# Seven products instead of eight in the last down projection of every feed-forward block

## The chip, the cores and the metric

One core of one Trainium2 chip runs the whole program. The metric is device time in microseconds (us); the kernel before takes 2784.4 us in the median of three runs (2784.36 to 2786.01). The profiled execution took 2784.26 us, of which the profile's span, from the first to the last instruction, is 2782.7 us.

## The reference

A trunk of two layers works on 640 tokens (512 of one new stream, 16 of each of eight running streams) with 1024 features. Every layer is

```python
x += 1/2 * SwiGLU_a(RMSNorm(x))        # hidden width 2816
x += mixer(RMSNorm(x))                 # layer 0: retention, layer 1: stick-breaking attention
x += 1/2 * SwiGLU_b(RMSNorm(x))
x += sigmoid(RMSNorm(x) @ W_gate) * (p[i] @ W_proj)
```

and a final RMSNorm follows. SwiGLU is `(silu(a) * b) @ w_down` with `a, b = split(x @ w_gu)`. All of it is float32.

## The kernel before

**Layout.** The residual stream `x` stays on the chip as eight tiles of 128 features by 640 tokens; a token half is 320 columns. A float32 matrix product is made of three passes over high and low parts: every operand is split by the scalar engine (high part, rounded, L1078 and the like) and the vector engine (low part, the difference), and the tensor engine multiplies high by high, high by low and low by high. One matmul instruction covers a 128x128 weight block and 320 columns. The phases are `ffn, ret, ffn, ple, ffn, sb, ffn, ple`: four feed-forward blocks, each followed by another kind of phase.

**A feed-forward block** runs through its 22 hidden tiles in groups of 4, 6, 6 and 6 (`PIECES`, L38). Each group makes its gate and up tiles and then adds its share of the down projection to `x`. In groups 1 to 3 the gate and up products go by Winograd's form of Strassen's scheme: seven products of quarter matrices instead of eight. Groups 1 and 2 do the same in the down projection (`SEVEN_DOWN`, L50). There a *job* (kind `dn`) is one pair of output tiles d and d+1: seven products of 9 matmuls each, so four jobs per group. Group 0 and, in this kernel, the last group do the down projection plainly: eight output tiles of 36 matmuls each (in the last group L751 to L755, a loop of two rounds).

**The order in a down job** is written by hand. With `d` the job, `old` the one before it and `new` the one after it, the tensor engine runs: product 1 of d, product 3 of old, 2 and 6 of d, 4 of old, 5 and 7 of d (L643 to L706). Product 2 waits for `snap1` (scalar engine, product 1 copied to a second bank), product 6 for `lo56` (vector engine, low parts of two weight sums), product 7 for `snap2`, product 3 for `lo34`, product 4 for `c22` (the first of the vector engine's four additions into `x`: c22, c11, c12, c21). The scalar engine's queue in a job is snap1, hi12 of new, snap2, hi34 of d, hi56 of new, hi7 of new (L1229 on). The vector engine's is c22 of old, lo56 and lo7 of d, c11 and c12 of old, the weight sums s1 to s3 of new, c21 of old, lo12 and s4 of new, lo34 of d (L1940 on). Each engine runs its queue in order.

**The hand-over to the next phase.** The last group's additions give the final `x`. In the plain form each finished tile is at once split for the next phase (`feed`, L1099: `feed_hi`, then `square`; `feed_lo` on the vector engine, L1732), and GpSimd adds the squares up in `ssum` (`add_squares`, L1593). The squares pass through the two-slot buffer `sq`, which lies over the end of the low parts of the hidden tiles. The next phase begins with matmuls on its slot-0 weights; these are split (`split_hi`, `split_lo`) at the end of the feed-forward block. Then `sum_squares` (L564) sums over the partitions, which needs all eight squares added. It stands behind 48 matmuls in `ret` and `sb` and behind 36 in `ple`, where the products with the layer's input embedding come first. `sb` starts only when every bank of the feed-forward block has been read.

Of the kernel before, what the change touches and what calls it, by code (L numbers as in the profile page):

```python
# [26 lines left out]
P = 128  # L27
D = 1024
KT = D // P
SEQ, STREAMS, STEP = 512, 8, 16  # L30
TOK = SEQ + STREAMS * STEP
# [15 lines left out]
LAST = len(PIECES) - 1  # L47


SEVEN_DOWN = (1, 2)  # L50
B11, T1, B21, T2, T3, B22, T4 = range(7)
JOBS = [FAST[n] + KT // 2 * (n in SEVEN_DOWN) for n in range(len(PIECES))]
PIECE_AT = [2 * sum(PIECES[:n]) + KT * n for n in range(len(PIECES))]
# [4 lines left out]
CREDIT = 4  # L58
# [145 lines left out]
def trunk(nc, phases, xT, pT, gains, wst, ones_d, ident_d, negtri_d, cs_d, dec_d, rmask_d, smask_d, gpow_d,  # L204
# [6 lines left out]
    with ctx:  # L211
# [41 lines left out]
            sq = sb("sq", [P, 2, TOK], F, s)  # L253
        with ExitStack() as s:

            sb("over_t2", [P, 2, 3, 4, HALF], F, s)
            sb("over_g_hi2", [P, 3 * 7 * HALF], F, s)
            g_raw = sb("g_raw", [P, 3, 7, HALF], F, s)
# [170 lines left out]
        def b_side(product, whole, extra):  # L429

            at_x = {1: (0, 0), 2: (1, 0), 3: (1, 1), 4: (0, 1)}
            return quarter(whole, *at_x[product]) if product < 5 else extra[:, product - 5, :, :]

        def g_tile(buf, k):

            return buf[:, k * TOK:(k + 1) * TOK]
# [37 lines left out]
        def jobs_of(c, piece):  # L474

            jobs = fast_pairs(c, piece)
            nxt = fast_pairs(c, piece + 1)[0] if piece in SEVEN_DOWN else None
# [61 lines left out]
        def _(pe):  # L539
# [45 lines left out]
            def ffn(c):  # L585
# [123 lines left out]
                for nf_at, nf in enumerate(PIECES):  # L709

                    if nf_at == 0:
                        for j in range(2 * PLAIN):
                            step(j, 0, 0, j < 4)
                            if j == 2 * PLAIN - 1:
                                by_quarters(j)
                            else:
                                project(c, j, 0, 0, (c["unit"] + 1 + j) % 4, [(k, k) for k in range(KT)],
                                        x_hi, x_lo, fed(c) if j == 0 else None)
                            if j == c["ss_after"]:
                                sum_squares(c)  # L720
                    else:
                        winograd(nf_at)
                    m += 2 * nf
                    done = c["g"] + sum(PIECES[:nf_at + 1])

                    def ready(b, nf=nf, done=done):
                        if b == 0:
                            pe.wait_ge(s_glo, CREDIT + done - 1)
                        if b == nf - 1:
                            pe.wait_ge(s_glo, CREDIT + done)  # L730
                    if nf_at == 0:

                        for d, blocks in ((0, range(nf - 1)), (1, range(nf - 2)), (0, (nf - 1,)), (1, range(nf - 2, nf))):
                            if blocks[0] == 0:
                                step(m + d, 0, 0)
                            p, u = (c["n"] + m + d) % 2, (c["unit"] + 1 + m + d) % 4
                            for k in blocks:
                                if d == 0:
                                    ready(k)
                                last = mm3(acc(u), w_hi[:, p, k * P:(k + 1) * P], w_lo[:, p, k * P:(k + 1) * P],  # L740
                                           g_tile(g_hi, k), g_tile(g_lo, k), k == 0, k == nf - 1)
                            if blocks[-1] == nf - 1:
                                last.then_inc(s_fill, 1)
                        for d in range(2, KT):
# [3 lines left out]
                    if nf_at != LAST:  # L748
                        m += KT
                        continue  # L750
# [322 lines left out]
        def _(act):  # L1073
# [19 lines left out]
            def square(c_fed, norm, d, s, value):  # L1093

                act.wait_ge(s, CREDIT + value)
                act.wait_ge(s_ssum, CREDIT + c_fed + d - 1)
                nc.scalar.activation(sq[:, d % 2, :], x[:, d, :], ACT.Square).then_inc(s_sq, 1)

            def feed(c_fed, norm, d, s, value):  # L1099

# [17 lines left out]
            def ffn(c):  # L1118
# [90 lines left out]
                def ghi(d):  # L1209
# [10 lines left out]
                    else:  # L1220
# [5 lines left out]
                        nc.scalar.activation(high[:, B22:T4 + 1, :], low[:, B22:T4 + 1, :],  # L1226
                                             ACT.Copy).then_inc(s_ghi, 1)

                def winograd(piece):  # L1229
                    for old, d, new in jobs_of(c, piece):  # L1230
                        made = old if old and old["kind"] == "gu" else None
# [12 lines left out]
                        if not old:  # L1244
                            hi1(new)
                            snap2(d)
                            hi2(new)
                        elif new:
                            hi12(new)
                        if made and made["seven"]:  # L1250
                            silu(made)
                            snap2(d)
                        elif old:
                            snap2(d)
                            if made:
                                silu(made)
                        hi34(d)
                        if made:
                            ghi(made)
                        if d["kind"] == "gu":  # L1260
                            snap3(d)
                        if new:
# [3 lines left out]
                            act.wait_ge(s_prod[5], CREDIT + d["q"] + 1)  # L1266
                            split_hi(c, d["m"], 0, 0, c["fill"] + d["m"])
                    if piece == LAST:
                        silu(d)
                        split_hi(c, d["m"] + 1, 0, 0, c["fill"] + d["m"] + 2)  # L1270
                        ghi(d)

                for nf_at, nf in enumerate(PIECES):
                    if nf_at == 0:
# [35 lines left out]
                        m += KT  # L1310
                        continue
                    for d in range(KT):
                        if nf_at < LAST and d >= KT - 2:
# [7 lines left out]
                        if nf_at == LAST:  # L1321
                            feed(c["fed"] + KT, c["norm"] + 1, d, s_free, o + m + d + 1)
                            if c["split_p"] and d == 4:
                                act.wait_ge(s_p, 16 * (c["ple"] + 1))
                                nc.scalar.activation(p_hi[:], p_raw[:], ACT.Copy).then_inc(s_phi, 1)
                    m += KT

            def ple(c):
# [260 lines left out]
        def _(pool):  # L1589
# [3 lines left out]
            def add_squares(fed, norm):  # L1593

                for d in range(KT - (norm == len(plan))):
                    pool.wait_ge(s_sq, CREDIT + fed + d + 1)
                    if d == 0:
                        pool.wait_ge(s_ss, CREDIT + norm)
                        nc.gpsimd.tensor_copy(ssum[:], sq[:, 0, :]).then_inc(s_ssum, 1)
                    else:  # L1600
                        pool.wait_ge(s_ssum, CREDIT + fed + d)
                        nc.gpsimd.tensor_tensor(ssum[:], ssum[:], sq[:, d % 2, :], ALU.add).then_inc(s_ssum, 1)

            def ffn(c):
                if c["split_p"]:
# [109 lines left out]
        def _(dve):  # L1715
# [46 lines left out]
            def ffn(c):  # L1762
# [177 lines left out]
                def winograd(piece):  # L1940
                    for old, d, new in jobs_of(c, piece):
# [19 lines left out]
                            continue  # L1961
                        if summed:
                            c11_c12(summed)
                            s1_s2(new)
                            s3(new)
                            c21(summed)
                            lo12(new)
                            s4(new)
# [26 lines left out]
                    if piece == LAST:  # L1995
                        c22(d)
                        split_lo(c, d["m"], 0, 0)
                        c12(d)
                        gated(d, 1)
                        gated(d, 0)  # L2000
                        split_lo(c, d["m"] + 1, 0, 0)
                        glo(d)

                for nf_at, nf in enumerate(PIECES):
                    gbase = c["g"] + sum(PIECES[:nf_at])
# [48 lines left out]
                    for d in range(KT):  # L2054
# [4 lines left out]
                        if nf_at == LAST or d < KT - 2:  # L2059
# [3 lines left out]
                        if nf_at == LAST:  # L2063
                            feed_lo(c["fed"] + KT, c["norm"] + 1, d)
                            if c["split_p"] and d == 4:
                                dve.wait_ge(s_phi, CREDIT + c["ple"] + 1)
                                tt(p_lo[:], p_raw[:], p_hi[:].bitcast(F), ALU.subtract).then_inc(s_plo, 1)
                        elif d == KT - 4:
# [597 lines left out]
```

## Time and profile before

| | |
|---|---|
| median of three runs | 2784.4 us |
| profiled execution: device time / span | 2784.26 us / 2782.7 us |
| tensor engine (matmuls) busy | 2744.7 us, 99% of the span |
| vector engine busy | 1920.1 us, 69% |
| scalar engine busy | 1207.2 us, 43% |
| GpSimd busy | 191.7 us, 7% |
| mean granted tensor-engine clock | 0.996 |
| chain that ended last | tensor engine 97%, vector engine 2% |

A share of busy time is a mean over very different stages. Matmuls overlap in the pipeline, so the duration that a row gives for one matmul is not the time by which it moves the next one; that is the distance between two starts. The profile's "idle before" of a matmul is counted from the modelled end of the one before it and is therefore shorter than the pause between starts.

### The profile page before, as it was taken

The numbers are of one execution on the slowest core, as the hardware profiler recorded it, in microseconds if no ns is written. First come the engines' busy times: TensorE is split into PE (matmuls) and PEld (weight loads), VectorE is DVE, ScalarE is ACT, GpSimd is POOL, SyncE is SP. The second block draws the span as 40 slices with busy tenths as digits, with TensorE's granted clock in tenths as the row PEclk, the third lists the DMA queues.
The fourth block names the chain that finished last, engine by engine and source line by source line (L and its number), as shares of the span: only waits on it lengthen the run. The fifth ranks groups of instructions, "written<-read, shape, count | busy, mean of one in ns | idle before, by whom it ended". The sixth has DMA issues, their size and how long they took to land.

```text
span 2782.7 us, 47474 instructions
## 1 busy us (share of the span) xinstructions
PE 2744.7 (99%) x18946; PEld 2699.7 (97%) x18946; DVE 1920.1 (69%) x2691; ACT 1207.2 (43%) x1629; POOL 191.7 (7%) x190
## 2 busy tenths in 40 slices
PE   8999999999999999999999999999999999999997
PEld 8999999999999999999999999999999999999997
DVE  7888864646464678888557788865555568888755
ACT  5445443323132444454444455444534443545443
POOL 0000003101010110000010000002000020000021
PEclk9999999999999999999999999999999999999998
DMA  3322323333232313323321222223222112232231
GB/s 120 95 84 79 97 79 124 110 103 114 92 110 95 104 55 94 87 81 92 93 76 60 85 85 87 88 84 121 88 83 91 68 61 72 77 101 77 86 99 53
DMA packets 80909, 246.96 MB, mean 89 GB/s; under 512 B 8465, under 2 KB 25121, under 8 KB 79681
## 3 DMA queue, kind: packets, MB, share of 16 engines
q1 hardware_dynamic: 71408, 204.67, 23.6%
q0 software_dynamic: 9296, 39.40, 3.9%
q8 instruction: 149, 2.44, 0.4%
q14 instruction: 56, 0.45, 0.1%
HBM read 226.74 MB, written 17.30 MB: 88 GB/s over the span
## 4 chain that ended last, share of the span: by engine, by line
PE 97%; DVE 2%; ACT 0%; issue 0%; DMA 0%; ACTq 0%; SPq 0%; DVEq 0%
PE ps L618 42%; PE ps L547 35%; PE ps L930 7%; PE ps L806 4%; PE ps L983 2%; PE ps L599 1%; PE ps L904 1%; PE ps L1017 1%; PE ps L967 1%; PE ps L871 1%; PE ps L855 0%; PE ps L1003 0%; PE ps L874 0%; PE ps L849 0%; PE ps L883 0%
## 5 line engine op out<-in xcount | busy, mean ns | idle before, releaser
L1086 ACT ACTIVATE w_hi<-raw 128x1024 fp32r<-128x1024 f32 (+2 forms) x210 | 201.3, 959 | 522.4 <-PE ps L547 382.3
L1729 DVE TENSOR_TENSOR w_lo<-raw,w_hi 128x1024 fp32r<-128x1024 f32 (+2 forms) x210 | 238.1, 1134 | 100.5 <-ACT w_hi L1086 97.5
L547 PE MATMUL ps<-x_hi,w_hi 128*128 128x320 f32 x1216 | 283.7, 315 | 9.7 <-DVE x_lo L1734 8.7
L547 PE MATMUL ps<-x_hi,w_lo 128*128 128x320 f32 x1216 | 277.6, 310 | 0.0
L547 PE MATMUL ps<-x_lo,w_hi 128*128 128x320 f32 x1216 | 277.4, 309 | 0.0
L547 PEld LDWEIGHTS ps<-x_hi,w_hi 128*128 128x128 f32 x1216 | 204.3, 188 | 13.5 <-DVE w_lo L2472 8.7
L547 PEld LDWEIGHTS ps<-x_lo,w_hi 128*128 128x128 f32 x1216 | 203.9, 188 | 0.0
L547 PEld LDWEIGHTS ps<-x_hi,w_lo 128*128 128x128 f32 x1216 | 203.7, 188 | 0.0
L1150 ACT ACTIVATE wx_hi<-raw 128x1024 fp32r<-128x1024 f32 (+1 forms) x92 | 92.4, 1004 | 252.4 <-PE ps L618 215.1
L618 PE MATMUL ps<-x_hi,w_hi 128*128 128x320 f32 x576 | 178.7, 310 | 0.0
L618 PE MATMUL ps<-x_hi,w_lo 128*128 128x320 f32 x576 | 177.9, 309 | 0.0
L618 PE MATMUL ps<-x_lo,wx_hi 128*128 128x320 f32 x576 | 177.8, 309 | 0.0
L618 PE MATMUL ps<-x_hi,wx_hi 128*128 128x320 f32 x576 | 177.7, 309 | 0.0
L618 PE MATMUL ps<-x_lo,w_hi 128*128 128x320 f32 x576 | 177.6, 308 | 0.0
L618 PE MATMUL ps<-x_hi,wx_lo 128*128 128x320 f32 x576 | 177.4, 308 | 0.0
L618 PE MATMUL ps<-t_hi,w_lo 128*128 128x320 f32 x576 | 177.1, 307 | 0.0
L618 PE MATMUL ps<-t_lo,w_hi 128*128 128x320 f32 x576 | 177.1, 307 | 0.0
L618 PE MATMUL ps<-t_hi,w_hi 128*128 128x320 f32 x576 | 177.0, 307 | 0.0
L547 PE MATMUL ps<-g_hi,w_hi 128*128 128x320 f32 x640 | 145.5, 308 | 0.0
L547 PE MATMUL ps<-g_hi,w_lo 128*128 128x320 f32 x640 | 145.4, 307 | 0.0
L547 PE MATMUL ps<-g_lo,w_hi 128*128 128x320 f32 x640 | 145.4, 308 | 0.0
L1826 DVE TENSOR_TENSOR wx_lo<-raw,wx_hi 128x1024 fp32r<-128x1024 f32 (+1 forms) x92 | 105.9, 1152 | 36.5 <-ACT wx_hi L1150 36.5
(310 smaller groups left out, 7714.4 us busy)
## 6 DMA issues: line engine op xcount, KB each, us to landing
raw<-wst SPq DMA_DIRECT2D x292, 512.0 KB, 3.6
raw<-wst SPq DMA_DIRECT2D x96, 384.0 KB, 3.2
raw<-wst SPq DMA_DIRECT2D x32, 256.0 KB, 2.6
s<-st_d POOLq DMA_DIRECT2D x8, 1024.0 KB, 5.1
sts_o<-s POOLq DMA_DIRECT2D x16, 512.0 KB, 3.3
rd<-dec_d POOLq DMA_DIRECT2D x8, 640.0 KB, 5.5
kc<-kc_d POOLq DMA_DIRECT2D x8, 512.0 KB, 4.3
vc<-vc_d POOLq DMA_DIRECT2D x8, 512.0 KB, 5.2
```

Source lines behind the costliest of these rows:

```text
L547: last = nc.tensor.matmul(out[:, h, :], a, b[:, HALF * h:HALF * (h + 1)], start=start and q == 0, stop=stop and q == 2, skip_group_check=True)
L599: last = nc.tensor.matmul(acc(u)[:, h, :], a[:, p, w], b[:, k, cols], start=n in (0, 2) and k % 4 == 0 and q == 0, stop=n in (1, 3) and k ...
L618: last = nc.tensor.matmul(out, a[:, w], b[:, k, :], start=start and k == 0 and q == 0, stop=k == end - 1 and q == 2, skip_group_check=True)
L806: last = nc.tensor.matmul(out, a, b[:, p, w], start=part == 0 and k == 0 and q == 0 and t % 2 == 0, stop=part == 1 and k == 3 and q == 2, ...
L871: last = nc.tensor.matmul(f[:, t * DV:(t + 1) * DV], sc[:, t, :], vn[:, t, :], start=True, stop=t == 0)
L904: return nc.tensor.matmul(z[:, z0:z0 + w], bk[rows, par, b * P:(b + 1) * P], bq[rows, par, b * P:end], start=start, stop=False, skip_group ...
L930: last = nc.tensor.matmul(ps[:, sb_banks(use)[0], 0:HALF], a, b[:, xb, cols], start=n == 0 and q == 0, stop=n == len(blocks) - 1 and q == 2)
L983: last = nc.tensor.matmul(z[:, z0 + P * (b2 - b):z0 + ZW[b]], tri[:, int(b2 > b), :], src[:, from_piece, from_col:from_col + ZW[b2]], star ...
L1086: nc.scalar.activation(w_hi[:, (c["n"] + m) % 2, 0:cols], raw[:, r, 0:cols], ACT.Copy).then_inc(s_whi, 1)
L1150: nc.scalar.activation(wx_hi[:, 0:2, 0:d["width"]], raw_blocks(c, d)[:, 0:4:3, :], ACT.Copy).then_inc(s_hi12, 1)
L1729: tt(w_lo[:, p, 0:cols], raw[:, r, 0:cols], w_hi[:, p, 0:cols].bitcast(F), ALU.subtract).then_inc(s_wlo, 1)
L1826: tt(wx_lo[:, 0:2, w], raw_blocks(c, d)[:, 0:4:3, :], wx_hi[:, 0:2, w].bitcast(F), ALU.subtract).then_inc(s_lo12, 1)
```

## The change

The last group's down projection takes the seven-product form too. It becomes four jobs; the plain loop goes. The weights of this group are stored in the paired form. Products 3 and 4 of the very last job stand alone at the end. The squares move into two new buffers over `t_lo`, which is free by then (`sq` would lie in the low parts that the jobs now read).

The feeding of the next phase follows the pairs. On the scalar engine, after hi34 of job d: feed_hi of both tiles of old, then both squares, then the weight work for new. On the vector engine, after lo34 of d: feed_lo of both tiles of old. After the last job the scalar engine does feed_hi of both final tiles, the split of the next phase's slot 1, then both squares; the vector engine does c22, the slot-0 split, c11, c12, c21, both feed_lo, the slot-1 split. The split of the ple input (`p_hi`, `p_lo`) moves into the last job.

```diff
-SEVEN_DOWN = (1, 2)
+SEVEN_DOWN = (1, 2, 3)
+            sb("over_t_hi2", [P, 3, 4, HALF], F, s)
+            sq_mix = sb("sq_mix", [P, 2, TOK], F, s)
+            sb("over_t_mid", [P, 3 * 4 * HALF - 4 * TOK], F, s)
+            sq_ple = sb("sq_ple", [P, 2, TOK], F, s)
...
-                    with pe.Fori(0, KT // 4) as i:
-                        for j in range(4):
-                            step(m + j, i, 4)
-                            project(c, m + j, i, 4, (c["unit"] + 1 + m + j) % 4, [(k, k) for k in range(nf)],
-                                    tiles(g_hi), tiles(g_lo), ready if j == 0 else None)
...
+                def fed(d):
+
+                    act.wait_ge(s_up, CREDIT + 2 * d["sum"] + 2)
+                    feed_hi(c["norm"] + 1, d["out"])
+                    act.wait_ge(s_free, CREDIT + o + d["m"] + 2)
+                    feed_hi(c["norm"] + 1, d["out"] + 1)
+
+                def square_of(n):
+                    square(c["fed"] + KT, c["norm"] + 1, n, s_xhi, c["fed"] + KT + n + 1)
...
+                        elif c["split_p"]:
+                            act.wait_ge(s_p, 16 * (c["ple"] + 1))
+                            nc.scalar.activation(p_hi[:], p_raw[:], ACT.Copy).then_inc(s_phi, 1)
...
                         hi34(d)
                         if made:
                             ghi(made)
+                        if piece == LAST and d["kind"] == "dn":
+                            fed(old)
+                            square_of(old["out"])
+                            square_of(old["out"] + 1)
...
                     if piece == LAST:
-                        silu(d)
+                        fed(d)
                         split_hi(c, d["m"] + 1, 0, 0, c["fill"] + d["m"] + 2)
-                        ghi(d)
+                        square_of(d["out"])
+                        square_of(d["out"] + 1)
...
                             lo34(d)
+                            if piece == LAST and d["kind"] == "dn":
+                                feed_lo(c["fed"] + KT, c["norm"] + 1, summed["out"])
+                                feed_lo(c["fed"] + KT, c["norm"] + 1, summed["out"] + 1)
                             continue
...
                     if piece == LAST:
                         c22(d)
                         split_lo(c, d["m"], 0, 0)
-                        c12(d)
-                        gated(d, 1)
-                        gated(d, 0)
+                        c11_c12(d)
+                        c21(d)
+                        feed_lo(c["fed"] + KT, c["norm"] + 1, d["out"])
+                        feed_lo(c["fed"] + KT, c["norm"] + 1, d["out"] + 1)
                         split_lo(c, d["m"] + 1, 0, 0)
-                        glo(d)
```

## Rows read from the trace of the kernel before

**Rows 1.** Chain of work that ended last, longest pieces: start, us, what.

```profile
175.54 110.64 PE ps L618 x753
...
392.56 49.28 PE ps L547 x336
```

**Rows 2.** Waits of the tensor engine: total us, times, longest.

```profile
PE ps L618 <- ACT ps L1195: 1.3, 8, 0.2
...
PE ps L930 <- DVE x L2058: 0.9, 1, 0.9
```

**Rows 3.** Timeline, tensor and scalar engine, group 2's first down job: start, us, instruction, [idle].

```profile
286.29 0.31 PE L618 MATMUL ps<-g_hi,wx_lo 128*128 128x320 f32 x1
286.77 0.38 PE L618 MATMUL ps<-g_hi,wx_hi 128*128 128x320 f32 x1 [0.16 <-ACT ps L1195]
...
286.20 0.42 ACT L1195 ACTIVATE ps<-ps 128x320 f32<-128x320 f32 x1 [1.15 <-PE ps L618]
```

**Rows 4.** Timeline, scalar engine, one down job of group 2.

```profile
304.25 0.84 ACT L1182 ACTIVATE w_hi<-raw 128x768 fp32r<-128x768 f32 x1 [0.96 <-PE ps L618]
305.56 0.85 ACT L1170 ACTIVATE w_hi<-w_sum 128x768 fp32r<-128x768 f32 x1 [0.46 <-PE ps L618]
306.89 0.53 ACT L1176 ACTIVATE wx_hi<-raw 128x384 fp32r<-128x384 f32 x1 [0.48 <-PE ps L618]
308.15 0.42 ACT L1187 ACTIVATE ps<-ps 128x320 f32<-128x320 f32 x1 [0.74 <-PE ps L618]
```

**Rows 5.** Busy time by stretch, group 2's down projection: us, then engines, PEclk, DMA.

```profile
282.00:318.80 36.80, 36.64 (x250) 36.40 (x249) 32.69 (x50) 17.88 (x28) 0.00 (x0) 1.00 0.29 85
```

**Rows 6.** Timeline, vector engine, the same job as Rows 4.

```profile
306.13 0.95 DVE L1854 TENSOR_TENSOR w_lo<-raw,w_hi 128x768 fp32r<-128x768 f32 x1
307.00 0.48 DVE L1861 SCALAR_TENSOR_TENSOR x<-ps,x 128x320 f32<-128x320 f32 x1
307.40 0.95 DVE L1843 TENSOR_TENSOR w_lo<-w_sum,w_hi 128x768 fp32r<-128x768 f32 x1
```

**Rows 7.** Timeline, GpSimd and vector engine, where the mixer of layer 0 ends.

```profile
983.38 1.67 POOL L1602 TENSOR_TENSOR ssum<-ssum,sq 128x640 f32<-128x640 f32 x1 [2.99 <-ACT sq L1097]
985.90 1.68 POOL L1602 TENSOR_TENSOR ssum<-ssum,sq 128x640 f32<-128x640 f32 x1 [0.85 <-ACT sq L1097]
...
983.51 0.81 DVE L2271 TENSOR_TENSOR x<-x,ps 128x640 f32<-128x640 f32 x1
984.28 1.85 DVE L1729 TENSOR_TENSOR w_lo<-raw,w_hi 128x1024 fp32r<-128x1024 f32 x1
986.06 2.20 DVE L1734 SCALAR_TENSOR_TENSOR x_lo<-x,gain,x_hi 128x640 fp32r<-128x640 f32 x1
```

**Rows 8.** Timeline, hand-over from the second feed-forward block to ple, by engine.

```profile
1407.12 1.06 ACT L1086 ACTIVATE w_hi<-raw 128x1024 fp32r<-128x1024 f32 x1 [2.87 <-PE ps L547]
1408.08 0.81 ACT L1090 ACTIVATE x_hi<-x,gain 128x640 fp32r<-128x640 f32 x1
1408.80 0.72 ACT L1097 ACTIVATE sq<-x 128x640 f32<-128x640 f32 x1
...
1408.21 1.23 DVE L1729 TENSOR_TENSOR w_lo<-raw,w_hi 128x1024 fp32r<-128x1024 f32 x1 [0.33 <-ACT w_hi L1086]
1409.35 0.88 DVE L1734 SCALAR_TENSOR_TENSOR x_lo<-x,gain,x_hi 128x640 fp32r<-128x640 f32 x1
...
1409.60 2.05 POOL L1602 TENSOR_TENSOR ssum<-ssum,sq 128x640 f32<-128x640 f32 x1 [3.22 <-ACT sq L1097]
...
1412.14 1.24 PE L570 MATMUL ps<-ssum,ones 128*128 128x320 f32 x4
```

**Rows 9.** Timeline, GpSimd, an addition of squares while the vector engine rests.

```profile
1442.32 1.58 POOL L1602 TENSOR_TENSOR ssum<-ssum,sq 128x640 f32<-128x640 f32 x1 [5.43 <-ACT sq L1097]
```

**Rows 10.** Tensor engine after its longest pause, timeline; then busy time by stretch.

```profile
725.48 0.28 PE L806 MATMUL ps<-w_lo,x_hi 128*128 128x256 f32 x1 [2.92 <-issue]
...
725.00:730.00 5.00, 4.52 (x26) 4.51 (x26) 0.00 (x0) 0.00 (x0) 0.00 (x0) 0.66 0.24 89
```

More of the change, by code:

```diff
@@ L254, in trunk @@
         with ExitStack() as s:
+            sb("over_t_hi2", [P, 3, 4, HALF], F, s)
+            sq_mix = sb("sq_mix", [P, 2, TOK], F, s)
+            sb("over_t_mid", [P, 3 * 4 * HALF - 4 * TOK], F, s)
+            sq_ple = sb("sq_ple", [P, 2, TOK], F, s)
+        with ExitStack() as s:
             sb("over_t2", [P, 2, 3, 4, HALF], F, s)
@@ L432, in b_side, with squares @@
             return quarter(whole, *at_x[product]) if product < 5 else extra[:, product - 5, :, :]
+        def squares(norm):
+            if norm == 0 or norm > len(phases) - 1 or phases[norm - 1] != "ffn":
+                return sq
+            return sq_ple if phases[norm] == "ple" else sq_mix
         def g_tile(buf, k):
@@ L476, in jobs_of @@
             jobs = fast_pairs(c, piece)
-            nxt = fast_pairs(c, piece + 1)[0] if piece in SEVEN_DOWN else None
+            nxt = fast_pairs(c, piece + 1)[0] if piece < LAST else None
             old = fast_pairs(c, piece - 1)[-1] if piece - 1 in SEVEN_DOWN else None
@@ L747, in ffn @@
                                     tiles(g_hi), tiles(g_lo))
-                    if nf_at != LAST:
-                        m += KT
-                        continue
-                    with pe.Fori(0, KT // 4) as i:
-                        for j in range(4):
-                            step(m + j, i, 4)
-                            project(c, m + j, i, 4, (c["unit"] + 1 + m + j) % 4, [(k, k) for k in range(nf)],
-                                    tiles(g_hi), tiles(g_lo), ready if j == 0 else None)
                     m += KT
@@ L1096, in square @@
                 act.wait_ge(s_ssum, CREDIT + c_fed + d - 1)
-                nc.scalar.activation(sq[:, d % 2, :], x[:, d, :], ACT.Square).then_inc(s_sq, 1)
+                nc.scalar.activation(squares(norm)[:, d % 2, :], x[:, d, :], ACT.Square).then_inc(s_sq, 1)
             def feed(c_fed, norm, d, s, value):
@@ L1312, in ffn @@
                     for d in range(KT):
-                        if nf_at < LAST and d >= KT - 2:
+                        if d >= KT - 2:
                             if d == KT - 2:
@@ L1320, in ffn @@
                         split_hi(c, m + d, 0, 0, c["fill"] + m + d + 1)
[L1321 to L1325, printed above, removed]
                     m += KT
@@ L1598, in add_squares @@
                         pool.wait_ge(s_ss, CREDIT + norm)
-                        nc.gpsimd.tensor_copy(ssum[:], sq[:, 0, :]).then_inc(s_ssum, 1)
+                        nc.gpsimd.tensor_copy(ssum[:], squares(norm)[:, 0, :]).then_inc(s_ssum, 1)
                     else:
                         pool.wait_ge(s_ssum, CREDIT + fed + d)
-                        nc.gpsimd.tensor_tensor(ssum[:], ssum[:], sq[:, d % 2, :], ALU.add).then_inc(s_ssum, 1)
+                        nc.gpsimd.tensor_tensor(ssum[:], ssum[:], squares(norm)[:, d % 2, :], ALU.add).then_inc(s_ssum, 1)
             def ffn(c):
@@ L1963, in winograd @@
                             c11_c12(summed)
-                            s1_s2(new)
-                            s3(new)
+                            if new:
+                                s1_s2(new)
+                                s3(new)
+                            elif c["split_p"]:
+                                dve.wait_ge(s_phi, CREDIT + c["ple"] + 1)
+                                tt(p_lo[:], p_raw[:], p_hi[:].bitcast(F), ALU.subtract).then_inc(s_plo, 1)
                             c21(summed)
-                            lo12(new)
-                            s4(new)
+                            if new:
+                                lo12(new)
+                                s4(new)
                             lo34(d)
+                            if piece == LAST and d["kind"] == "dn":
+                                feed_lo(c["fed"] + KT, c["norm"] + 1, summed["out"])
+                                feed_lo(c["fed"] + KT, c["norm"] + 1, summed["out"] + 1)
                             continue
@@ L2058, in ffn @@
                         stt(out=xd, in0=acc(u), scalar=0.5, in1=xd, op0=ALU.mult, op1=ALU.add).then_inc(s_free, 1)
-                        if nf_at == LAST or d < KT - 2:
+                        if d < KT - 2:
                             split_lo(c, m + d, 0, 0)
@@ L2062, in ffn @@
                             t_low((6, 1, 2, 3, 4)[d], 3 + d)
[L2063 to L2068, printed above, removed]
+                        if d == KT - 4:
                             first = fast_pairs(c, nf_at + 1)[0]
```

## Prediction

> **What bounds the kernel now.** The order of reading is chain, waits of the tensor engine, then the timelines of the stages that the change touches. The chain is almost only matmuls, in pieces without a break: 753 matmuls in 110.64 us, 336 in 49.28 us [rows 1]. So the tensor engine is the bound, and both forms of the down projection already run at 0.147 us per matmul (110.64/753, 49.28/336). This is the price of a matmul here, not the 0.31 us that a row gives for one [rows 3]: matmuls overlap, and who takes the duration doubles the gain. The list of waits shows what little is lost: 1.3 us in eight waits on L1195 (snap2 of the first job of a seven-product down group), 0.9 us at the start of sb [rows 2].
>
> The second thing to see is how full the vector engine is beside it. In the down projection of group 2 it works 32.69 of 36.80 us [rows 5], 1.0 us free per job of 9.25 us (63 matmuls). The change puts work exactly there.
>
> **The change, part by part.** I cost one feed-forward block. The last group's four jobs are laid over the timeline of group 2's jobs, which is the same work; the added instructions are queued in the program's order with the durations of the rows, instructions of one engine following each other 0.09 us before the reported end (1408.08 to 1408.80 for one of 0.81) [rows 8].
>
> *Matmuls.* 288 become 252: 36 x 0.147 = 5.3 us less.
>
> *First job.* Product 7 waits for snap2, as in groups 1 and 2. The starts are 286.29 and 286.77, so 0.48 - 0.15 = 0.33 us is lost (the profile's 0.16 counts from the modelled end) [rows 3]. The plain form had nothing of the kind here: its 336 matmuls run through [rows 1]. +0.3. The loop that becomes straight code and the weights in two blocks of the same size I cost at nothing: groups 1 and 2 do both inside an unbroken piece [rows 1]. If the code had to be waited for, it would be about the 2.9 us that the one such pause takes [rows 10].
>
> *Scalar engine, jobs 2 and 3.* In group 2 snap1 starts at 308.15, 3.9 us after hi34 (304.25), with 0.46, 0.48 and 0.74 us of waiting between [rows 4]. The change puts two feed_hi (0.73 each) and two squares (0.63 each) behind hi34. From 304.25: 0.75 + 1.46 + 1.26 + 0.76 + 0.45 = 308.9, then 0.42 for snap1, and 0.15 until the tensor engine follows a copy (286.62 to 286.77) [rows 3]. Product 2 could begin four products after hi34's own release, at about 309.3; it begins at 309.5. 0.2 us in each of two jobs: +0.4.
>
> *Vector engine, jobs 2 and 3.* Two feed_lo per job (0.79 each in a row, 0.88 alone [rows 8]) are 1.6 us, 0.6 more than is free; that alone stays within the 2.2 us that product 6 has to spare (below). But the additions on GpSimd now fall into this full queue, and the two engines exclude each other. Rows 7 show how. The addition of 983.38 leaves an operation with one operand in PSUM alone (0.81 us beside it). A split of 1024, 1.23 us otherwise [rows 8], is issued at 984.28 and takes 1.85: it ends 1.08 us after the addition does (985.05). The next addition is issued at 985.90, while that split runs, and ends 1.45 us after it (986.13 to 987.58). The feed_lo queued behind the split at 986.06 takes 2.20 instead of 0.88: the waiting addition went first [rows 7]. So each addition takes about 1.4 us of vector time whenever the queue is full of operations with two operands on the chip. The Trainium skill (SBUF — State Buffer, Who interferes with whom) states the same of every vector instruction with two SBUF inputs against a GpSimd instruction that reads SBUF; by it the weight sums and splits of the jobs, which no row shows beside an addition, are held like the two kinds shown, which would leave my sum as it is.
>
> In job 3 this stands in the path: lo34, then the addition of the first square (1.42), feed_lo (0.68 after it), the second addition (1.43), feed_lo (0.68), then c22 (0.40) and lo56 (0.95): lo56 ends 5.5 us after lo34 does, against 1.3 us in group 2 (307.08 to 308.35) [rows 6]. Product 6 starts two products (2.64 us) after snap1's release (308.15 - 0.2) there, at 310.6: 2.2 us to spare, so it waits about 2.1; with the 0.2 us by which lo34 itself falls behind the tensor engine, 2.3. In job 2 the first of the two is a copy of half the length and lo56 is late by less: 0.5. Together +2.8. If the additions did not hold the vector engine this term would be 0; if they held it in job 3 alone, 2.3.
>
> *Last job.* c22 comes behind both feed_lo; product 4 waits 0.2. +0.2. The split of the ple input, now in this job, costs nothing: lo34 behind it waits for hi34 anyway.
>
> Inside the group: -5.3 + 0.3 + 0.4 + 2.8 + 0.2 = -1.6 us.
>
> *Hand-over.* Count from the end of product 4 of job 2 (time 0). The tensor engine runs products 5, 7, 3, 4 of the last job until 5.5. The scalar engine: hi34 from 0.25, two feed_hi, two squares, and only then the slot-0 split, 3.7 to 4.8. The low part follows, 4.85 to 6.15, so the next phase can begin at 6.2: 0.75 us lost. The vector engine goes on with c11, c12 (to 7.7) and c21 (to 8.1); feed_hi of the last two tiles 7.8 to 9.3, the slot-1 split to 10.3, the squares to 10.9 and 11.5. The first addition waits for the vector engine's slot-1 split and ends at 13.0; the second, with the vector engine at rest, takes 1.58 [rows 9] and ends at 14.7; sum_squares can run at 14.8.
>
> - ret: 48 matmuls from 6.2 end at 13.25. Lost 0.75 + 1.5 = 2.25; before, nothing.
> - sb: starts after c21 at 8.2, 2.7 lost, against 1.1 before (the 0.9 of [rows 2] counted between starts). Its 48 matmuls end at 15.2, later than 14.8. +1.6.
> - ple, twice: one product waits 0.2 for c21; 36 matmuls from 6.2 end at 11.7, so sum_squares waits 3.05. Lost 0.75 + 0.2 + 3.05 = 4.0. Before, the last addition ended at 1411.65 and sum_squares began at 1412.14, in line [rows 8]: the cover was just enough, and it goes.
>
> GpSimd's transfers for ret and sb are queued behind these additions and start about 2 us later against sum_squares. What needs them comes after the mean square and, on the tensor engine, after 48 matmuls more (7 us): I take nothing; 0 to 2 us each is what a wrong cover could cost.
>
> *Sum.* ret -1.6 + 2.25 = +0.7; sb -1.6 + 1.6 = 0.1 (rounded from the unrounded terms); ple 2 x (-1.6 + 4.0) = +4.9. Total +5.7 us on 2784.26 us of the profiled execution (span 2782.7), which is within 0.2 us of the median: **2790 us**.
>
> **A pause and the clock.** After the longest pause of the trace (2.92 us, and a shorter one before it) the granted clock is 0.66 over five us, so part of it at the lower level, 1.2 GHz instead of 2.4: 0.34 x 5 = 1.7 us lost [rows 10]. The pause before sum_squares in ple is 3.05 us between starts, 2.9 as the profile counts. The Trainium skill (TensorE: Matmul & The Clock Gate, HAM oscillation) warns that idle gaps bring the lower clock back. My sum leaves it out, since matmuls stand close on both sides here; with it, up to 2 x 1.7 = 3.4 us more.
>
> **The rivals.**
> - *The vector engine is not held* (it goes first, or GpSimd finds gaps). Against it: both additions of rows 7. For it: in the down jobs a third of the operations read PSUM and leave room. The hand-overs stay; 4 x 2.8 and half a us of additions go: 2790 - 11.7 = 2778.4. Faster by 0.2%. It decides from the point at which lo56 is less than 2.2 us late. Chance 0.17.
> - *The clock falls in both ple hand-overs*: 2790 + 3.4 = 2793. Chance 0.18.
> - *Nothing new stands in the path*: 4 x (-5.3 + 0.3) = -20, 2764. It needs the squares to be ready 3 us earlier than the queue order allows. Chance 0.05.
> - *More is late than I see* (code, transfers in sb): 2796. Chance 0.05.
>
> **How the numbers follow.** Forecast 2790, chance 0.55; its own bounds are 2787 to 2793 (0.1 us on each of some six steps per block). The range is 2777 to 2796; it leaves out the full gain and little else. A measurement of this kernel can tell 0.2%, 5.6 us, from no change. The forecast lies on that bound, so half of it counts as slower, half as no change. Slower: 0.27 + 0.16 + 0.05 = 0.48. Within: 0.28 + 0.02 + 0.07 = 0.37. Faster: 0.10 + 0.05 = 0.15.
>
> **What would show it.** Matmuls of the last group at L618, 144 fewer in all. In each last group a wait of product 6 on L1843 of about 2 us, and x_lo rows (L1734) of about 2.2 us beside additions. Waits on the slot-0 split at the start of ret and ple, on c21 in sb, and of about 3 us at L570 before sum_squares in ple, 1.5 in ret. Granted clock at 1.00 after them. The forecast is wrong if L1843's wait is missing (then the first rival), or if the clock is lower behind L570 (the second).

## The result, and the profile after

| | before | after |
|---|---|---|
| median of six runs | 2784.42 us | 2796.26 us |
| lowest, highest | 2784.26, 2786.01 | 2791.14, 2797.28 |
| profiled execution: span, mean granted clock | 2782.7 us, 0.996 | 2789.6 us, 0.995 |
| matmuls | 18946 | 18802 |

The ratio is 1.0037, 95% interval 1.0024 to 1.0050: slower by 0.4%, with 144 matmuls fewer. Five of the six runs lie between 2794.4 and 2797.3; the one that was profiled is the shortest, 2791.14 (span 2789.6).

The first view of after is the list of the tensor engine's waits (total us, times, longest). L630 is the matmul of a product (L618 before), L559 that of a projection, L582 sum_squares, L934 a projection of sb.

```profile
PE ps L630 <- DVE w_lo L1860: 9.6, 8, 2.1
...
PE ps L582 <- POOL ssum L1619: 6.8, 3, 2.8
PE ps L559 <- issue: 2.5, 3, 1.0
PE ps L934 <- DVE x L1905: 2.5, 1, 2.5
...
PE ps L630 <- ACT ps L1199: 2.0, 12, 0.2
...
PE ps L559 <- DVE w_lo L1746: 1.1, 2, 0.5
```

Three lines have no counterpart in the list of before, from which [rows 2] is taken: 9.6 us on lo56 (L1860), 6.8 us on the additions and 1.1 us on the slot-0 split (at the start of both ple). The wait on snap2 has gone from 8 to 12 times, and that at the start of sb from 0.9 to 2.5 us. These are the waits that were forecast; the one on the slot-0 split at the start of ret stands under "issue" (0.58 us at 434.21).

The second view places the waits: the chain that ended last (start, us, what). First before, then after. The x753 piece is group 1, the x4 piece sum_squares of the next phase; so the distance from the one to the other is one feed-forward block's end and its hand-over. The first start of before, 175.54, stands in [rows 1].

```profile
441.84 1.08 PE ps L570 x4
...
1147.77 110.64 PE ps L618 x753
1412.30 1.08 PE ps L570 x4
...
1645.60 110.64 PE ps L618 x753
1913.07 1.08 PE ps L570 x4
...
2431.83 110.64 PE ps L618 x753
2696.36 1.08 PE ps L570 x4
...
2698.40 65.38 PE ps L547 x444
```

```profile
175.46 110.64 PE ps L630 x753
...
442.76 1.31 PE ps L582 x4
...
1145.40 110.64 PE ps L630 x753
...
1412.66 1.31 PE ps L582 x4
...
1647.49 110.64 PE ps L630 x753
...
1916.62 1.08 PE ps L582 x4
...
2433.70 110.64 PE ps L630 x753
...
2702.47 1.31 PE ps L582 x4
...
2704.75 66.86 PE ps L559 x444
```

| group 1 to sum_squares, us | before | after | difference | forecast | with the pauses filled (below) |
|---|---|---|---|---|---|
| into ret | 266.30 | 267.30 | +1.00 | +0.7 | +0.95 |
| into the first ple | 264.53 | 267.26 | +2.73 | +2.45 | +2.71 |
| into sb | 267.47 | 269.13 | +1.66 | +0.1 | +0.17 |
| into the second ple | 264.53 | 268.77 | +4.24 | +2.45 | +2.73 |
| sum | | | +9.63 | +5.7 | +6.56 |

The two large misses, sb and the second ple, are 1.5 us each above the last column. The same size shows behind sum_squares in the last ple: the same 444 matmuls take 66.86 us instead of 65.38. The third view says what it is. The busy times by stretch (us, then the engines, the granted clock, DMA) of the profiled execution of after:

```profile
1415.00:1420.00 5.00, 5.00 (x26) 5.00 (x27) 4.90 (x7) 2.50 (x3) 0.00 (x0) 0.72 0.02 3
...
1910.00:1915.00 5.00, 5.00 (x28) 5.00 (x27) 1.14 (x1) 1.13 (x2) 4.28 (x4) 0.73 0.33 105
...
2685.00:2690.00 5.00, 5.00 (x28) 5.00 (x27) 3.48 (x5) 2.48 (x4) 0.00 (x0) 0.74 0.24 93
...
2705.00:2710.00 5.00, 5.00 (x26) 5.00 (x27) 4.90 (x7) 2.32 (x3) 0.00 (x0) 0.70 0.02 3
```

The tensor engine is busy throughout, yet does 26 to 28 matmuls in 5 us and not the 34 of 0.147 us: part of each stretch ran at the lower of the two clocks, 1.2 GHz. Each of the four stretches follows one of the new pauses: sum_squares of the first ple (2.76 us), the start of sb (2.51), product 6 in the last job ahead of the second ple (2.10) and its sum_squares (2.75). So the clock fell four times here, 1.3 to 1.5 us each.

Elsewhere the profiled execution of after is shorter than before's: from sum_squares in ret to the next block by 3.29 us (the pause of [rows 10] is 0.6 us instead of 2.92 and the clock does not fall behind it), in sb by 1.68 (before has a granted clock of 0.80 and 0.85 over ten us from 2245, after has not) and in the final norm by 0.93. With 9.63 and the 3.25 us more behind the two sums of ple that makes 6.98 (9.63 + 3.25 - 3.29 - 1.68 - 0.93), against the 6.9 by which the spans differ (a start 0.08 us earlier is the rest).

### The profile page after: what moved, and what is told of

Its sections match the earlier page's. It is cut to its first block, busy times and chain, and to the rows that moved or that the text cites. A ratio compares the mean times of both kernels' runs of the same rounds, so it can differ in the third digit from the quotient of the medians.

```text
span 2789.6 us, 47598 instructions
## 1 busy us (share of the span) xinstructions
PE 2733.0 (98%) x18802; PEld 2681.8 (96%) x18802; DVE 2029.7 (73%) x2871; ACT 1245.8 (45%) x1709; POOL 195.2 (7%) x190
## 3 DMA queue, kind: packets, MB, share of 16 engines
q8 instruction: 153, 2.51, 0.4%
## 4 chain that ended last, share of the span: by engine, by line
PE 92%; DVE 4%; issue 1%; ACT 1%; POOL 0%; DMA 0%; SPq 0%; ACTq 0%; DVEq 0%; POOLq 0%
PE ps L630 45%; PE ps L559 28%; PE ps L934 7%; PE ps L810 4%; PE ps L987 2%; DVE x_lo L1751 1%; PE ps L611 1%; PE ps L908 1%; PE ps L1021 1%; PE ps L971 1%; PE ps L875 1%; PE ps L859 0%; PE ps L1007 0%; POOL ssum L1619 0%; PE ps L878 0%
## 5 line engine op out<-in xcount | busy, mean ns | idle before, releaser
L1090 ACT ACTIVATE w_hi<-raw 128x1024 fp32r<-128x1024 f32 (+1 forms) x178 | 174.2, 979 | 418.9 <-PE ps L559 288.9
L559 PE MATMUL ps<-x_hi,w_hi 128*128 128x320 f32 x1216 | 283.6, 315 | 10.2 <-DVE x_lo L1751 8.6
L559 PE MATMUL ps<-x_hi,w_lo 128*128 128x320 f32 x1216 | 277.6, 309 | 0.0
L559 PE MATMUL ps<-x_lo,w_hi 128*128 128x320 f32 x1216 | 277.5, 309 | 0.0
L1746 DVE TENSOR_TENSOR w_lo<-raw,w_hi 128x1024 fp32r<-128x1024 f32 (+1 forms) x178 | 207.3, 1165 | 93.4 <-ACT w_hi L1090 92.9
L1154 ACT ACTIVATE wx_hi<-raw 128x1024 fp32r<-128x1024 f32 (+1 forms) x104 | 102.5, 985 | 280.0 <-PE ps L630 243.9
L559 PEld LDWEIGHTS ps<-x_hi,w_hi 128*128 128x128 f32 x1216 | 204.1, 188 | 14.5 <-DVE w_lo L2492 8.4
L559 PEld LDWEIGHTS ps<-x_hi,w_lo 128*128 128x128 f32 x1216 | 203.8, 188 | 0.0
L559 PEld LDWEIGHTS ps<-x_lo,w_hi 128*128 128x128 f32 x1216 | 203.7, 188 | 0.0
L630 PE MATMUL ps<-g_hi,w_hi 128*128 128x320 f32 x576 | 179.1, 311 | 9.7 <-DVE w_lo L1860 9.6
L630 PE MATMUL ps<-x_hi,w_hi 128*128 128x320 f32 x576 | 178.7, 310 | 0.0
L630 PE MATMUL ps<-x_hi,w_lo 128*128 128x320 f32 x576 | 178.0, 309 | 0.0
L630 PE MATMUL ps<-g_lo,w_hi 128*128 128x320 f32 x576 | 177.8, 309 | 0.0
L630 PE MATMUL ps<-x_lo,wx_hi 128*128 128x320 f32 x576 | 177.8, 309 | 0.0
L630 PE MATMUL ps<-g_hi,w_lo 128*128 128x320 f32 x576 | 177.8, 309 | 0.0
L630 PE MATMUL ps<-x_hi,wx_hi 128*128 128x320 f32 x576 | 177.8, 309 | 0.0
L630 PE MATMUL ps<-x_lo,w_hi 128*128 128x320 f32 x576 | 177.6, 308 | 0.0
L630 PE MATMUL ps<-x_hi,wx_lo 128*128 128x320 f32 x576 | 177.4, 308 | 0.0
L630 PE MATMUL ps<-t_lo,w_hi 128*128 128x320 f32 x576 | 177.1, 307 | 0.0
L630 PE MATMUL ps<-t_hi,w_lo 128*128 128x320 f32 x576 | 177.1, 307 | 0.0
L630 PE MATMUL ps<-t_hi,w_hi 128*128 128x320 f32 x576 | 177.0, 307 | 0.0
L1843 DVE TENSOR_TENSOR wx_lo<-raw,wx_hi 128x1024 fp32r<-128x1024 f32 (+1 forms) x104 | 117.3, 1128 | 42.9 <-ACT wx_hi L1154 42.9
```

What stands on the lines that cost most here:

```text
L559: last = nc.tensor.matmul(out[:, h, :], a, b[:, HALF * h:HALF * (h + 1)], start=start and q == 0, stop=stop and q == 2, skip_group_check=True)
L630: last = nc.tensor.matmul(out, a[:, w], b[:, k, :], start=start and k == 0 and q == 0, stop=k == end - 1 and q == 2, skip_group_check=True)
L1090: nc.scalar.activation(w_hi[:, (c["n"] + m) % 2, 0:cols], raw[:, r, 0:cols], ACT.Copy).then_inc(s_whi, 1)
L1154: nc.scalar.activation(wx_hi[:, 0:2, 0:d["width"]], raw_blocks(c, d)[:, 0:4:3, :], ACT.Copy).then_inc(s_hi12, 1)
L1746: tt(w_lo[:, p, 0:cols], raw[:, r, 0:cols], w_hi[:, p, 0:cols].bitcast(F), ALU.subtract).then_inc(s_wlo, 1)
L1843: tt(wx_lo[:, 0:2, w], raw_blocks(c, d)[:, 0:4:3, :], wx_hi[:, 0:2, w].bitcast(F), ALU.subtract).then_inc(s_lo12, 1)
```

## The experiments

The kernels stand against the changed kernel: 2796.26 us above and 2796.04 in the second series. The kernel before, run beside each series, stays at 2784.2 to 2784.4 us.

**1. The additions moved, the work the same.**

```diff
+ jobs = [d for _, d, _ in jobs_of(c, LAST)] if norm and c["kind"] == "ffn" else None
  for d in range(...):
      pool.wait_ge(s_sq, CREDIT + fed + d + 1)
+     if jobs and d in (0, 2):
+         pool.wait_ge(s_wlo, CREDIT + c["n"] + jobs[d // 2 - 2]["m"] + 1)
```

> The changed kernel with two waits more on GpSimd: the additions of tiles 0 and 1 wait until the vector engine has done lo7 of the third job, those of tiles 2 and 3 until lo7 of the last job, so that they fall beside c11 and c12, which read PSUM, and behind lo56. The work is the same. Theory (the additions hold the vector engine in front of lo56): the waits of product 6 on lo56 (9.6 us in eight waits) go, minus 10 to 11 us; 2796.3 us becomes 2785, and 2784 or less if a fall of the clock behind these waits goes with them. Rival (the queue is too full by the feed_lo alone, whoever adds when): the waits stay and the time stays at 2796. Second rival (the held time only moves to the hand-over): the waits on lo56 go, and those on the slot-0 split and sum_squares grow by as much.

Measured: 2784.06 us median of 11 runs (2781.59 to 2786.12), ratio to before 1.0001 (0.9992 to 1.0010). Two waits on GpSimd are worth 12 us, where 10 to 11 were expected. The timeline of the vector engine, GpSimd and the tensor engine in the third and the last job ahead of the first ple:

```profile
1379.21 0.82 DVE L1899 SCALAR_TENSOR_TENSOR x<-ps,x 128x640 f32<-128x640 f32 x1
1380.07 0.82 DVE L1903 SCALAR_TENSOR_TENSOR x<-ps,x 128x640 f32<-128x640 f32 x1
1380.81 1.47 DVE L1829 TENSOR_TENSOR w_sum<-raw 128x384 f32<-128x384 f32 x1
...
1392.93 1.81 DVE L1875 TENSOR_TENSOR w_lo<-raw,w_hi 128x768 fp32r<-128x768 f32 x1
1394.67 2.98 DVE L1755 SCALAR_TENSOR_TENSOR x_lo<-x,gain,x_hi 128x640 fp32r<-128x640 f32 x2
...
1380.29 1.57 POOL L1623 TENSOR_TENSOR ssum<-ssum,sq_ple 128x640 f32<-128x640 f32 x1
1389.53 4.39 POOL L1623 TENSOR_TENSOR ssum<-ssum,sq_ple 128x640 f32<-128x640 f32 x2 [7.67 <-DVE wx_lo L1870]
1395.04 4.02 POOL L1623 TENSOR_TENSOR ssum<-ssum,sq_ple 128x640 f32<-128x640 f32 x2 [1.11 <-ACT sq_ple L1101]
...
1398.10 0.41 PE L630 MATMUL ps<-g_hi,w_hi 128*128 128x320 f32 x1 [1.72 <-DVE x L1882]
```

The addition of 1380.29 leaves c12 (L1903), whose other operand is in PSUM, at 0.82 us, and holds the weight sum behind it (1.47 instead of the 0.55 in group 2 of before). The wait on lo56 is gone from the list. Some of the held time did move, though to product 4 and not, as the second rival had it, to the slot-0 split and sum_squares: in ple the additions of tiles 2 and 3 hold lo34 (1.81 instead of 0.95) and hardly the split of the input (1.57 instead of 1.48), so the feed_lo of tiles 4 and 5 come later, where an addition holds them (2.98 for two instead of 1.68). c22 stands behind them and product 4 waits 1.72 us, where the changed kernel shows no such wait. So the listed waits account for 6.7 of the 12 us: 9.6 us on lo56 and 1.0 at sum_squares are gone, 3.9 on c22 and lo34 are new. The rest was not traced; with the pauses of product 6 the falls of the clock behind them went too, one in the first profile of after and two in the second (experiment 6). The Trainium skill (SBUF — State Buffer, Who interferes with whom) has the rule that an instruction of the vector engine with two inputs in SBUF contends with a GpSimd instruction that reads SBUF, and one with at most one such input, outside its two-port modes, does not; these rows agree, also for weight sums and splits of the jobs, which no row of before showed.

**2. The same additions made short.** The first six additions work on one column.

```diff
+ w = 1 if d < KT - 2 and norm and plan[norm - 1]["kind"] == "ffn" else TOK
- nc.gpsimd.tensor_tensor(ssum[:], ssum[:], squares(norm)[:, d % 2, :], ALU.add)
+ nc.gpsimd.tensor_tensor(ssum[:, 0:w], ssum[:, 0:w], squares(norm)[:, d % 2, 0:w], ALU.add)
```

> The changed kernel, but the additions of tiles 0 to 5 of every norm behind a feed-forward block work on one column instead of 640 (the other 639 columns of these squares are left out of the mean square); all waits and signals stay. Theory (it is the length of the additions that holds the vector engine): the waits on lo56 go (9.6 us), the rows of x_lo take 0.88 us, and the time is 2784 to 2786, as with the additions moved. Rival (the vector engine is late because GpSimd's access as such disturbs it, or because of the feed_lo alone): less than 4 us is gained. Product 4 of the last job should wait 0.2 us as predicted, not 1.7 us as with the additions moved, because no addition then falls beside the last two feed_lo.

Measured: 2779.84 us (2777.19 to 2780.92, 11 runs), ratio 0.9982 (0.9973 to 0.9991); 4 to 6 us better than expected. The same place in the timeline, first in the changed kernel (into ret), then here (into ple):

```profile
419.33 3.82 POOL L1619 TENSOR_TENSOR ssum<-ssum,sq_mix 128x640 f32<-128x640 f32 x2 [6.86 <-ACT sq_mix L1101]
...
419.52 4.32 DVE L1751 SCALAR_TENSOR_TENSOR x_lo<-x,gain,x_hi 128x640 fp32r<-128x640 f32 x2
...
425.16 0.41 PE L630 MATMUL ps<-g_hi,w_hi 128*128 128x320 f32 x1 [2.10 <-DVE w_lo L1860]
```

```profile
1385.21 1.48 POOL L1621 TENSOR_TENSOR ssum<-ssum,sq_ple 128x1 f32<-128x1 f32 x2 [7.97 <-ACT sq_ple L1101]
...
1384.97 1.68 DVE L1754 SCALAR_TENSOR_TENSOR x_lo<-x,gain,x_hi 128x640 fp32r<-128x640 f32 x2
```

Two feed_lo take 1.68 us instead of 4.32 (which is their time in the changed kernel ahead of ple too), and no wait on lo56 or c22 is left, not even the 0.2 us expected at product 4. It is the additions and not the number of feed_lo that makes lo56 late. That this kernel is 4 us below the first one fits the wait of product 4 there, 3.5 us in two.

**3. The last two additions made short**, tiles 6 and 7 (the same edit with `d >= KT - 2`).

> The changed kernel, but the additions of tiles 6 and 7 of every norm behind a feed-forward block add one column instead of 640 (the other 639 columns of the last two squares are left out of the mean square); all waits and signals stay. Theory (sum_squares waits for the last two additions): its pauses of 2.76 us in both ple and 1.27 us in ret go, minus 6.8 us, and with them the matmuls at the lower clock that follow in ple (1.5 us each): 2796.3 us becomes 2786 to 2790. Rival (the squares, not the additions, are late): the pauses stay above 1.5 us and the time within 2 us of 2796.

Measured: 2784.67 us (2782.38 to 2787.03), ratio 1.0001 (0.9992 to 1.0010): 11.6 us gained, 1.3 more than the most that was expected; 6.8 of them are the waits. All pauses of sum_squares are gone from the waits, and the 9.7 us on lo56 stand as they were. So the two costs have separate places.

**4. The sum later in ple.** The work is the same, the pause is given cover.

```diff
- if d == 2:
+ if n == PLE_SS - 1:                  # PLE_SS = 6
+     pe.wait_ge(s_free, CREDIT + c["unit"] + PLE_SS - 3)
      sum_squares(c)
...
- mean_square(c)
  for d in range(KT):
+     if d == PLE_SS:
+         mean_square(c)
```

> The changed kernel, with sum_squares of ple after six products of the input's projection instead of three (its bank takes the place of the seventh unit, and the reading of the mean square stands behind six copies of the vector engine). Theory (the pause is only a want of cover): both pauses of 2.76 us go, and the 0.2 us on c21, and the clock does not fall behind them (1.5 us each): 2796.3 us becomes 2787 to 2790. Rival (the chain from the sum to the reciprocal root is then too late for the first gate): the pause moves to the gates' banks, and the time stays within 2 us of 2796.

Measured: 2782.37 us (2779.84 to 2783.67, 11 runs), ratio 0.9995 (0.9985 to 1.0004): 13.9 us, 4.6 more than the most that was expected. What I had not counted is a second pause: 0.96 us behind sum_squares of each ple, "issue" in the list of waits. Two of the three waits of that line in the changed kernel are these (the third, 0.58 us, is at the start of ret); here one of 0.6 is left, that of ret. Before has the pause as well:

```profile
PE ps L547 <- issue: 1.9, 2, 1.0
```

The profile names no releaser. By the program the next product of the projection writes into the bank that the reading of the mean square (L1757) frees, and the rows of after stand in that order:

```profile
2703.83 0.82 DVE L1757 TENSOR_SCALAR scr<-ps 128x640 f32<-128x640 f32 x1 [4.57 <-PE ps L582]
...
2704.75 0.87 PE L559 MATMUL ps<-p_hi,w_hi 128*128 128x320 f32 x2 [0.96 <-issue]
```

With 2 x (2.76 + 0.2 + 0.96) and two falls of 1.5 us it makes 10.8; for the other 3 us I have no row.

**5. The pauses filled.** Matmuls without use run in the pauses; no wait becomes shorter.

```diff
+ for _ in range(12):                  # ahead of product 6 of the last job
+     nc.tensor.matmul(d["y"], ..., start=True, stop=True, skip_group_check=True)
  pe.wait_ge(s_lo56, CREDIT + d["q"] + 1)
...
+ spare(acc(u), ..., 18)               # ahead of sum_squares in ple; 8 in ret; 12 at the start of sb
  pe.wait_ge(s_ssum, CREDIT + c["fed"] + KT)
```

> The changed kernel, with matmuls of no use in the tensor engine's pauses: 12 in front of product 6 of the last job, 18 in front of sum_squares in ple, 8 in ret, 12 at the start of sb. No wait becomes shorter. Theory (the runs differ by how often the clock falls after a pause): the granted clock stays at 1.00 through the four hand-overs, the runs agree to 1 us, and the time is 2796.3 less the falls, 2787 to 2790. Rival (the spread of the runs has another cause): median 2796 and a spread of 5 us, as without the added matmuls.

Measured: 2786.68 us (2784.91 to 2787.49, 11 runs), ratio 1.0008 (0.9999 to 1.0017). Useless work makes the kernel 9.6 us faster. The granted clock of the stretches that stood at 0.70 to 0.74 in the first profile of after:

```profile
1415.00:1420.00 5.00, 5.00 (x37) 5.00 (x35) 4.90 (x7) 1.92 (x3) 0.00 (x0) 1.00 0.00 0
...
1910.00:1915.00 5.00, 5.00 (x33) 4.68 (x32) 0.00 (x0) 0.00 (x0) 4.86 (x7) 1.00 0.55 172
...
2685.00:2690.00 5.00, 4.98 (x34) 4.64 (x32) 4.23 (x7) 4.21 (x6) 2.15 (x2) 1.00 0.34 103
...
2705.00:2710.00 5.00, 5.00 (x37) 5.00 (x36) 4.93 (x7) 0.00 (x0) 0.00 (x0) 1.00 0.15 45
```

Its starts in the chain (175.78 to 443.03, 1144.80 to 1412.04, 1645.60 to 1913.24, 2431.99 to 2699.25) give the last column of the table above: what the change costs there without the clock. The runs still differ by 2.6 us, more than the 1 us I had expected; what moves them was not measured.

**6. The changed kernel again.**

> The changed kernel itself, once more, beside the kernel before and the three kernels of this group, as the measure for the experiments. Expected: 2796 us against 2784, in most runs a granted clock of 0.993 to 0.995; the profile shows the clock fallen behind the pauses of some of the four hand-overs, not the same ones in each run.

Measured: 2796.04 us (2792.83 to 2797.11, five runs), ratio 1.0039 (1.0026 to 1.0053). This time an execution of 2796.04 was profiled, one at the median, and its clock fell in all four hand-overs:

```profile
425.00:430.00 5.00, 4.67 (x21) 4.67 (x22) 2.43 (x5) 0.56 (x2) 0.00 (x0) 0.66 0.34 108
...
1415.00:1420.00 5.00, 4.04 (x15) 3.49 (x14) 4.17 (x6) 1.57 (x2) 0.00 (x0) 0.59 0.01 3
1420.00:1425.00 5.00, 5.00 (x27) 5.00 (x27) 4.00 (x6) 1.06 (x1) 0.00 (x0) 0.73 0.14 33
...
1910.00:1915.00 5.00, 3.99 (x17) 3.99 (x18) 3.84 (x5) 3.75 (x5) 1.57 (x2) 0.66 0.34 107
...
2690.00:2695.00 5.00, 5.00 (x28) 5.00 (x28) 3.48 (x5) 2.59 (x4) 0.00 (x0) 0.75 0.24 96
...
2710.00:2715.00 5.00, 5.00 (x26) 5.00 (x26) 4.90 (x8) 2.21 (x3) 0.00 (x0) 0.70 0.01 3
```

The first line is the one to look at. It follows a pause of 2.10 us ahead of product 6. In the first profile of after the same pause, of the same 2.10 us, is followed by a clock of 1.00 over the same stretch:

```profile
425.00:430.00 5.00, 4.84 (x33) 4.84 (x34) 3.58 (x7) 2.26 (x4) 0.00 (x0) 1.00 0.32 108
```

**7. Both edits, and three more.** First experiments 1 and 4 together; then also the additions of tiles 4 and 5 behind the slot-0 split, sum_squares two blocks into k0 in ret, and other banks for the first q and v in sb.

```diff
+     if jobs and d == 4:
+         pool.wait_ge(s_wlo, CREDIT + c["n"] + FFN_SLOTS + 1)
...
- return (2 * "qkv".index(use[0]) + use[2] if use[1] == 0 else use[2],)
+ return (2 * "vkq".index(use[0]) + use[2] if use[1] == 0 else use[2],)
...
-     fed(c) if use == "q0" else None)
- if use == "q0":
-     sum_squares(c)
+     fed(c) if use == "q0" else lambda b: sum_squares(c) if b == 2 else None)
```

> Both edits at once: the additions of tiles 0 and 1 behind lo7 of the third job and those of 2 and 3 behind lo7 of the last, and sum_squares of ple after six products of the input's projection. If the two costs are separate, the gains add up: 2796.3 - 12.2 - 13.9 = 2770 us; if the clock's falls were counted in both, 2773. Rival (the second is only the first, passed on): no better than the better of the two, 2782.

> As the kernel with both edits, and three more: the additions of tiles 4 and 5 wait until the slot-0 split is done; in ret sum_squares stands two blocks into k0 instead of in front of it (its pause of 1.27 us is covered; the reciprocal root has 1.9 us to spare there); in sb the first projections of q and v change banks, so that q0 needs not wait for c21 (2.5 us, of which some 2 us come back as waits on the last two x_lo). Theory: 1.7 us less in both ple (the wait of product 4 on c22), 1.3 us in ret, 0.5 us in sb, and the fall of the clock in sb and ret: 2764 to 2768 us. Rival (the additions then hold the slot-1 split and the last x_lo as long): no better than the kernel with both edits.

Measured: 2773.35 us (2772.32 to 2774.64, five runs), ratio 0.9959 (0.9946 to 0.9973), and 2766.73 us (2764.33 to 2767.38, five runs), ratio 0.9933 (0.9919 to 0.9946). Against 2796.04 in the same series the two edits together gain 22.7 us, where the sum of the single gains is 26.1: the two costs are mostly separate, and the result is the 2773 that was named for falls of the clock counted in both. With both edits seven products are 0.41% faster than the kernel before, with three more 0.67%. That is not the worth of seven products alone: the plain form was not run with the later sum or the other banks, and it has pauses there too (1.9 us behind the two sums of ple, 0.9 at the start of sb). The three added edits were run only together. The largest of the hand-over's waits in the list of the last kernel are these (L641 is a product, L944 a projection of sb, L593 sum_squares):

```profile
PE ps L944 <- DVE x_lo L1767: 1.2, 1, 1.2
...
PE ps L641 <- DVE x L1894: 0.8, 2, 0.4
...
PE ps L593 <- POOL ssum L1635: 0.4, 2, 0.2
```

## Why the prediction was right, and where it was not

The side and the mechanism of the waits were right: slower, since the hold of the vector engine and the late sum cost more than 144 matmuls give. 2790 was forecast against the profiled execution; that of after took 2791.14. That these agree to 1 us is luck, for it was the shortest of the runs and a term left out of the sum met gains elsewhere (below). The median, 2796.26, lies just above the range's upper end, 2796: 11.8 us more than before, where 5.7 were forecast. The term left out is the fall of the clock. By the prediction's own sign (a lower clock behind L570) its second rival holds, not its forecast of 1.00. Step by step:

- **The matmuls** cost 0.147 us each, 144 fewer of them run, and the pieces of after still have this pitch (110.64/753).
- **First job.** The wait on snap2 came four times more, as counted (12 instead of 8).
- **Scalar engine.** The 0.2 us on snap1 is hardly seen: one wait of 0.2 us in the list, ahead of sb. In the last job ahead of ret product 2 starts at 421.50, 0.28 us after the matmul before it, so 0.13 is lost.
- **Vector engine held.** Forecast: waits of product 6 of 2.1 us in the last job and about 0.5 in the third. Measured: 2.10 (1.46 ahead of sb) and 0.46, 9.6 us in all. The price of 1.42 us per addition was read off two rows of another stage, and two feed_lo came out at 4.32 us where 1.68 is their length. Experiments 1 and 2 show that this term is caused by the additions; the rival without a hold is out.
- **Slot-0 split, c21, sum_squares.** Forecast 0.75 between starts into ret and ple; the rows have 0.58 and 0.5 from the modelled ends. Forecast 2.7 between starts in sb, listed 2.51. Forecast 3.05 and 1.5 at sum_squares, listed 2.76 and 1.27. The expected lines are there, each at its place.
- **The sum of these** came out at +6.56 us in the kernel with filled pauses, against +5.7. About 0.2 us per block is in no step of mine.
- **The clock** is the step that was sized wrong. I had set the falls at 2 x 1.7 us, only in the two ple, and gave them a chance of 0.18; the sum left them out. They come behind pauses of 2.1 and 2.5 us as well, thus in all four hand-overs, in the second ple twice. Most cost 1.2 to 1.6 us each: of the matmuls behind the pause a dozen or so follow each other by 0.27 us instead of 0.147. Experiment 5 takes them away together and gains 9.6 us of the median. Beside its profile the one at the median is longer by 8.5 us where the clock fell: 1.57 into ret, 2.68 behind the sum of the first ple, 1.44 into sb, 1.54 into the second ple and 1.22 behind its sum. Another 1.0 us lies between ret's sum and the next block, the part with the pause of [rows 10]. The row that I should have used better is my own, [rows 10]: I took its 2.92 us for a border, where it was one example. Of the six pauses of over 2 us, five were followed by a fall in the execution at the median; five times 1.5 us on top of the sum are 2797.5.
- **What hid it.** The profiled execution came within 1 us of 2790 because about 6 us were gained elsewhere: the pause of [rows 10], a fall of the clock in sb and the final norm. That pause differs between executions, even of one kernel (0.6 and 0.9 us in the two profiles of after, 0.4 to 1.2 or not listed in the other kernels); why was not tried.
- **GpSimd's transfers** were costed at nothing. No wait on them is new in the list, which agrees; the cost alone was not measured.

## What to carry to other kernels

In this kernel an addition on GpSimd was not free beside a vector engine full of operations with two operands on the chip: place it by a wait beside operations that read PSUM. Two waits gave back 12 us here, without any work taken away. A saved matmul was worth its pitch, a new pause of two or three us its length and, in most cases, another 1.5 us or so at the lower clock; a sum that is not needed at once should stand where other matmuls cover it.

## What the runs showed of the hardware

- The clock fell from 2.4 to 1.2 GHz behind pauses of 2.1 to 2.8 us, not each time: the same pause of 2.10 us was followed by 1.00 in one execution and 0.66 in another. In experiment 1 it fell behind shorter ones too, the 1.72 us of product 4 and 0.51 us two us later (0.67 from 1398 to 1403), and not behind the same pair ahead of the second ple (1.73 and 0.52 us, 1.00 from 2685 to 2690). It did not fall at once: in the second profile of after the matmuls behind the pause of 2.10 us follow each other by 0.15 us from 425.58 to 426.02 and by 0.27 from 426.25 to 429.18. The Trainium skill (TensorE: Matmul & The Clock Gate, HAM oscillation) describes waits between bursts that bring the lower clock back again and again; the runs agree on the effect, and add that one and the same kernel does it four times in one execution and five times in another.
- An addition of one column on GpSimd still took about 0.7 us (1.48 for two), but left the vector engine's feed_lo at 0.84 us each (1.68 for two).
